# Tiles of h and f set 448 columns apart in SBUF, with the decoding states of the feed-forward convolution in the gaps

## The reference

```
h = rmsnorm(x, g_mix_pre); z = h @ w_in            # 1024 -> 24 column tiles and the gates
a = conv group (GLU, causal conv of width 31, group LayerNorm, silu)
hm = mLSTM group (4 heads, chunkwise)
x = x + rmsnorm(concat([a, hm]) @ w_out, g_mix_post)
up = rmsnorm(x, g_ffn_pre) @ w_up                  # 1024 -> 2 x 2816
up, ffn_buf_new = causal_dwconv(up, ffn_buf, w_conv_ffn, b_conv_ffn)   # width 3
f = gelu(up[..., :D_FF]) * up[..., D_FF:]
x = x + rmsnorm(f @ w_down, g_ffn_post)
x = x + (p @ w_ple) * sigmoid(rmsnorm(x, g_ple) @ w_ple_gate)
```

## Time and profile before

| | us |
|---|---|
| median of 3 runs (2684.24 to 2689.28) | 2686.83 |
| the profiled execution | 2685.84 |
| its span, first to last instruction | 2684.0 |
| PE busy, share of the span | 2655.4, 99% |
| PE's weight loads busy | 2581.4, 96% |
| DVE, ACT, POOL busy | 1726.9, 921.4, 237.1 |
| mean granted clock of TensorE | 0.998 |
| matmuls of L732 | 12960 |

### The profile page before, as it was taken

One profiled execution on the slowest core, in us unless ns is written; L12 is line 12 of the kernel. 1 busy time (PEld: TensorE's weight loads), 2 busy tenths in 40 slices (PEclk: granted clock), 3 DMA queues, 4 the chain that ended last, 5 costly groups with the idle time before them and its releaser, 6 DMA issues.

```text
span 2684.0 us, 37676 instructions
## 1 busy us (share of the span) xinstructions
PE 2655.4 (99%) x14541; PEld 2581.4 (96%) x14541; DVE 1726.9 (64%) x3699; ACT 921.4 (34%) x1932; POOL 237.1 (9%) x180
## 2 busy tenths in 40 slices
PE   9999999999999999999999999999999999999999
PEld 7989999999999999999999999999999998899998
DVE  7985898865566666555675664756866636472645
ACT  5464434464332122344321233542112425311113
POOL 4433515140000000000000000000000000000000
PEclk9999999999999999999999999999999999999999
DMA  9867999877566666565666666466666575466665
GB/s 331 321 222 293 359 335 365 315 282 285 188 233 233 233 234 234 216 239 210 227 233 233 234 234 256 182 226 233 229 233 232 216 284 146 179 240 229 235 233 204
DMA packets 125117, 660.59 MB, mean 246 GB/s; under 512 B 22010, under 2 KB 22654, under 8 KB 55182
## 3 DMA queue, kind: packets, MB, share of 16 engines
q1 hardware_dynamic: 111150, 628.29, 63.8%
q10 hardware_dynamic: 13792, 29.92, 3.3%
HBM read 533.04 MB, written 125.11 MB: 245 GB/s over the span
## 4 chain that ended last, share of the span: by engine, by line
PE 93%; DVE 4%; ACT 2%; DMA 1%; issue 1%; SPq 0%; DVEq 0%; ACTq 0%
PE proj L732 85%; PE m L732 1%; PE m L899 1%; PE m L932 1%; PE m L933 1%; PE m L893 1%; PE m L910 0%; PE m L761 0%; DMA w_split<-w_kept 0%; DVE small L1994 0%; PE m L952 0%; PE m L705 0%; PE m L704 0%; PE m L706 0%; PE m L865 0%
## 5 line engine op out<-in xcount | busy, mean ns | idle before, releaser
L732 PE MATMUL proj<-h_split,w_split 128*128 128x416 f32 x8112 | 1562.8, 352 | 4.5 <-DVE h_split L1831 2.1
L732 PEld LDWEIGHTS proj<-h_split,w_split 128*128 128x128 f32 x8112 | 1505.7, 188 | 20.1 <-issue 7.8
L732 PE MATMUL proj<-f_split,w_split 128*128 128x416 f32 x4584 | 880.8, 352 | 7.7 <-DMA w_split<-w_kept 2.2
L732 PEld LDWEIGHTS proj<-f_split,w_split 128*128 128x128 f32 x4584 | 851.5, 188 | 28.1 <-DVE f_split L2042 4.4
L1874 DVE SCALAR_TENSOR_TENSOR cv<-a_ext,vecs,cv 128x416 f32<-128x416 f32 (+1 forms) x480 | 302.5, 677 | 0.0
L1536 ACT ACTIVATE temp_room<-proj 128x416 f32<-128x416 f32 x176 | 91.3, 519 | 547.4 <-PE proj L732 547.3
L688 POOL TENSOR_TENSOR w_split<-w_raw,w_split 128x512 fp32r<-128x512 f32 x174 | 234.3, 1368 | 368.2 <-ACT w_split L1112 368.2
L2346 DVE SCALAR_TENSOR_TENSOR m<-temp_room,vecs,m 128x416 f32<-128x416 f32 (+1 forms) x440 | 256.8, 652 | 0.0
L2376 DVE TENSOR_TENSOR f_split<-m,f_split 128x416 fp32r<-128x416 f32 x110 | 65.1, 592 | 233.4 <-ACT f_split L1548 233.4
L2343 DVE TENSOR_SCALAR m<-temp_room,vecs 128x416 f32<-128x416 f32 (+1 forms) x220 | 145.9, 709 | 65.6 <-ACT temp_room L1536 65.5
L1750 DVE TENSOR_TENSOR mix_room<-mix_room,temp_room 128x416 f32<-128x416 f32 x131 | 81.0, 618 | 102.9 <-ACT temp_room L1130 97.2
(11 more groups left out here) (288 smaller groups left out, 1975.0 us busy)
## 6 DMA issues: line engine op xcount, KB each, us to landing
w_split<-w_kept SPq DMA_DIRECT2D x430, 1024.0 KB, 4.8
w_kept<-w_split SPq DMA_DIRECT2D x107, 1024.0 KB, 6.5
w_raw<-in_w_units SPq DMA_DIRECT2D x216, 256.0 KB, 4.7
x_resid<-in_x ACTq DMA_DIRECT2D x5, 1664.0 KB, 12.0
out_y<-x_resid ACTq DMA_DIRECT2D x8, 832.0 KB, 8.6
rows<-in_x ACTq DMA_DIRECT2D x4, 832.0 KB, 7.4
w_raw<-in_x ACTq DMA_DIRECT2D x3, 832.0 KB, 9.0
qkv<-in_p ACTq DMA_DIRECT2D x5, 416.0 KB, 5.9
```

What stands on the lines that cost most here:

```text
L732: ins = mm(to, home[:, low_w, b * P:b * P + P], act[:, n, low_a, :], start=n == 0 and not low_w and not low_a, stop=n == len(blocks) - 1 a ...
```

## The change

All 16 tiles of h, the 11 high tiles of f and its low tiles 0 to 4 begin 448 columns apart (`STEP`); f's low tiles 5 to 7 and 8 to 10 stay 416 apart. h grows from 6880 to 7168 columns, f from 9152 to 9632. The buffer `up_dec` (704 columns) is gone: the states of tile pairs 0 to 15 lie in the 16 gaps of h, those of 16 to 21 in the first six gaps behind f's high tiles. So the states are loaded by two DMAs of 16 and 6 pieces of 128 bytes per partition, and stored by two, where it was one of 2816 bytes per partition each way. What lay in f's room from high tile 8 on now begins at column 8 x 448. Every buffer behind f starts elsewhere: h by 1920 bytes, the weights and what follows by 3072 bytes.

```diff
+STEP = T + ROOM
...
-        f = Tiles(f_flat, [j * T for j in range(FH)], [(j + (2 * FH - KD if j < KD else FH - KD)) * T for j in range(FH)])
-        f_room = sb("f_room", [P, FH * 2 * T])
-        h_room = sb("h_split", [P, (KD - 1) * (T + ROOM) + T + KD * T], F32R)
-        h = Tiles(h_room, [k * (T + ROOM) for k in range(KD)], [(KD - 1) * (T + ROOM) + (k + 1) * T for k in range(KD)])
+        f_low, apart = FH * STEP, 4
+        f_size = f_low + (FH - KD) * T + apart * STEP + (KD - apart) * T
+        f = Tiles(f_flat, [j * STEP for j in range(FH)],
+                  [f_low + (FH - KD + j) * T + min(j, apart) * ROOM if j < KD else f_low + (j - KD) * T for j in range(FH)])
+        f_room = sb("f_room", [P, f_size])
+        f_late = KD * STEP
+        h_room = sb("h_room", [P, 2 * KD * STEP])
+        h = Tiles(h_flat, [k * STEP for k in range(KD)], [(KD + k) * STEP for k in range(KD)])
...
-        up_dec = sb("up_dec", [P, FT, 2, DEC_B, 2])
+        in_h = 2 * KD
+        up_dec_h = h_room[:, :].rearrange("p (j e) -> p j e", e=STEP)[:, :, T:]
+        up_dec_f = f_room[:, 0:(FT - in_h) * STEP].rearrange("p (j e) -> p j e", e=STEP)[:, :, T:]
...
+        def up_states(tensor):
+
+            flat = tensor.rearrange("p j n b r -> p j (n b r)")
+            return ((up_dec_h, flat[:, 0:in_h]), (up_dec_f, flat[:, in_h:FT]))
...
-                    final(t["up_s"], up_dec[:, :, :, :, :])
+                    for home, states in up_states(t["up_s"]):
+                        final(states, home)
...
-            for name, home in state_homes:
-                act.dma_start(home, t[name]).then_inc(s_states.sem, 16)
+            for home, states in state_homes:
+                act.dma_start(home, states).then_inc(s_states.sem, 16)
...
-                            ins = fn(dec[:, n, :, 0:2], up_dec[:, j, n, :, :], ACT.Copy)
+                            ins = fn(dec[:, n, :, 0:2], up_dec(j)[:, n, :, :], ACT.Copy)
...
-                            v.tensor_copy(up_dec[:, j, n, :, :], dec[:, :, DEC_S:])
+                            v.tensor_copy(up_dec(j)[:, n, :, :], dec[:, :, DEC_S:])
```

More of the change, by code:

```diff
@@ L301, in signal @@
             return Signal(ctx.enter_context(nc.semaphore(name)), per, ring, unit)
-        with nc.sbuf_tensor("f_split", [P, FH * 2 * T], F32R) as f_flat:
-            pass
-        f = Tiles(f_flat, [j * T for j in range(FH)], [(j + (2 * FH - KD if j < KD else FH - KD)) * T for j in range(FH)])
-        f_room = sb("f_room", [P, FH * 2 * T])
-        h_room = sb("h_split", [P, (KD - 1) * (T + ROOM) + T + KD * T], F32R)
-        h = Tiles(h_room, [k * (T + ROOM) for k in range(KD)], [(KD - 1) * (T + ROOM) + (k + 1) * T for k in range(KD)])
+        f_low, apart = FH * STEP, 4
+        f_size = f_low + (FH - KD) * T + apart * STEP + (KD - apart) * T
+        with nc.sbuf_tensor("f_split", [P, f_size], F32R) as f_flat:
+            pass
+        f = Tiles(f_flat, [j * STEP for j in range(FH)],
+                  [f_low + (FH - KD + j) * T + min(j, apart) * ROOM if j < KD else f_low + (j - KD) * T for j in range(FH)])
+        f_room = sb("f_room", [P, f_size])
+        f_late = KD * STEP
+        with nc.sbuf_tensor("h_split", [P, 2 * KD * STEP], F32R) as h_flat:
+            pass
+        h_room = sb("h_room", [P, 2 * KD * STEP])
+        h = Tiles(h_flat, [k * STEP for k in range(KD)], [(KD + k) * STEP for k in range(KD)])
         w = sb("w_split", [P, RING, 2, KD * P], F32R)
@@ L329, in hymba_layer, with up_dec @@
         up_tail = sb("up_tail", [P, FT, 2, 2])
-        up_dec = sb("up_dec", [P, FT, 2, DEC_B, 2])
+        in_h = 2 * KD
+        up_dec_h = h_room[:, :].rearrange("p (j e) -> p j e", e=STEP)[:, :, T:]
+        up_dec_f = f_room[:, 0:(FT - in_h) * STEP].rearrange("p (j e) -> p j e", e=STEP)[:, :, T:]
+        def up_dec(j):
+            piece = up_dec_h[:, j, :] if j < in_h else up_dec_f[:, j - in_h, :]
+            return piece.rearrange("p (n b r) -> p n b r", n=2, b=DEC_B)
+        def up_states(tensor):
+            flat = tensor.rearrange("p j n b r -> p j (n b r)")
+            return ((up_dec_h, flat[:, 0:in_h]), (up_dec_f, flat[:, in_h:FT]))
         vecs = sb("vecs", [P, NVEC])
@@ L345, in hymba_layer @@
         mixf = out_room[:, 4 * T:8 * T].rearrange("p (c t) -> p c t", c=4)
-        conv_tok = f_room[:, KD * T:KD * T + CT * 4 * P].rearrange("p (c n e) -> p c n e", c=CT, e=P)
+        conv_tok = f_room[:, f_late:f_late + CT * 4 * P].rearrange("p (c n e) -> p c n e", c=CT, e=P)
         w_raw_room = w_raw[:, :, :].rearrange("p r e -> p (r e)")
@@ L361, in hymba_layer @@
         c_homes = (mix_room[:, 1680:1680 + DEC_B * E1], rows[:, 0:4, :].rearrange("p r t -> p (r t)")[:, 0:DEC_B * E1],
-                   w_raw_room[:, 0:DEC_B * E1], f_room[:, KD * T:KD * T + DEC_B * E1])
+                   w_raw_room[:, 0:DEC_B * E1], f_room[:, f_late:f_late + DEC_B * E1])
         c_dec = [home.rearrange("p (b e) -> p b e", e=E1) for home in c_homes]
@@ L384, in hymba_layer @@
         x_next_w = w_raw_room[:, 0:4 * T].rearrange("p (r t) -> p r t", t=T)
-        sq_next = (mix_room[:, 4 * T:5 * T], mix_room[:, 6 * T:7 * T], f_room[:, (KD + 5) * T:(KD + 6) * T])
+        sq_next = (mix_room[:, 4 * T:5 * T], mix_room[:, 6 * T:7 * T], f_room[:, f_late + 5 * T:f_late + 6 * T])
         def x_next(i, mid=False):
@@ L428, in hymba_layer @@
         ahead = G_OUT + 3
-        ahead_home = f_flat[:, KD * T:KD * T + 2 * KD * P].rearrange("p (s e) -> p s e", s=2)
+        ahead_home = f_flat[:, f_late:f_late + 2 * KD * P].rearrange("p (s e) -> p s e", s=2)
         def split_home(u):
@@ L540, in hymba_layer @@
         n_const, n_late = 2, 4 + 2 * len(MASK_ROWS) + len(PIECES)
-        state_homes = (("up_dec", up_dec[:, :, :, :, :]), ("a_dec", a_dec[:, :, :, 0:CW - 1]))
+        state_homes = up_states(t["up_dec"]) + ((a_dec[:, :, :, 0:CW - 1], t["a_dec"]),)
         block = ctx.enter_context(nc.Block())
@@ L673, in _ @@
                 final(t["y"][last_blk, :, first:end], x[:, first:end, :])
-            sp.wait_ge(s_end.sem, 16 * (6 + len(Y_PIECES)))
+            sp.wait_ge(s_end.sem, 16 * (7 + len(Y_PIECES)))
             sp.wait_ge(s_yout.sem, s_yout.done(last_blk - 1, 1))
```

## The result

| | before | changed |
|---|---|---|
| median of the runs, us | 2687.73 (2684.24 to 2690.84, 16 runs) | 2693.64 (2688.45 to 2698.04, 16 runs) |
| ratio, 95% interval | 1 | 1.0019 (1.0012 to 1.0026) |
| profiled execution, us | 2685.84 | 2694.41 |
| its span, us | 2684.0 | 2692.6 |

The changed kernel is slower by 5.9 us, 0.2%, where 2679.0 us was forecast. That is small, but the interval leaves out 1, and the time lies above the range's end of 2687.

A forecast was written before the change was run, and what follows sets the result against it. PE's matmul stream, busy 99% of the span, was taken as the bound. Savings of 3.6 + 0.05 + 4.1 = 7.8 us, other costs 0, gave 2679.0 us against the median; range 2674 to 2687.

The forecast's parts named there:

- h, 2736 x 1.33 ns = 3.6 us less: h's matmuls on low tiles, a third of 8208, each save 1.33 ns by moving from 416 to 448 columns apart.
- a: Time of one PE matmul in sweeps over tiles 448 columns apart, reckoned at 186.85 ns.
- The distance: PE's sweeps over h and f: tiles 448 columns apart run 1.33 ns faster per matmul than tiles 416 apart.
- f, 4.1 us less: f's matmuls on high tiles and low tiles 0 to 4, 3808 in all, gain from 448; 4.2 to 5.1 us, taken as 4.1.
- The jumps between the sweeps: f's steps between high and low tiles: part of f's excess belongs to them and stays.
- Alignment against the weights: Rival: h's high and low tiles fall together with the weights modulo 256 bytes and slow; at most 33 us, 2716 us; chance 0.05.
- No change: Rival: distance is not the cause; 2686.8 us, up to 3 us less; chance 0.17, 0.25 with partial gain below measurement.
- Late loads: Rival: small state-store pieces delay the last weight loads, PE waits 3.3 us near the end; 2682.3 us; chance 0.08.
- the issue on ACT: Loading the states at the start: three DMAs for two keep ACT busy 0.83 us longer, hidden in 4.91 us idle; cost 0.
- the copies: ACT and DVE instructions reading and writing the states stay the same in number and size; cost 0.
- The bounds of 0.8 and 0.5 us: Upper costs: 0.8 us for loading states on ACT without cover, 0.5 us PE wait near the end from storing them.

The follow-up runs named there:

- e9: e6 with h's room placed ahead of f's, so h's high tiles lie 128 bytes off the weights modulo 256; 2687.70 us, ratio 0.9995.
- e6: The changed kernel with h's low tiles 416 columns apart again, its high tiles still 448 apart and level with the weights; 2695.82 us, ratio 1.0022.
- e10: The kernel before with 32 empty columns (128 bytes) ahead of the weights, h and f unmoved; 2692.25 us, ratio 1.0017.
- e1: The changed kernel with h's room placed ahead of f's, so h lies 128 bytes off the weights; 2692.65 us, ratio 1.0014.
- e3: The changed kernel with rooms ordered weights, f, h; f's high tiles level with the weights, h 128 bytes off; 2706.18 us, ratio 1.0062.
- e4: e1 with f's low tiles 0 to 3 moved on by 32 columns; 2690.48 us, ratio 1.0005.
- e13: e1 run again unaltered; 2692.15 us.
- e14: e1 run a third time unaltered; 2690.77 us.
- e16: e4 run again unaltered; 2693.39 us.
- e7: e9 with f's low tiles 0 to 3 moved on by 32 columns as in e4; 2684.35 us, ratio 0.9985.
- e15: e7 with 8 empty columns (32 bytes) ahead of the weights; 2734.64 us, ratio 1.0175.
- e8: The changed kernel with all of h's low tiles 32 columns nearer, still 448 apart; high tiles level, low ones 128 bytes off; 2695.98 us, ratio 1.0027.

## Why the prediction was wrong

The step that failed is the term "h, 2736 x 1.33 ns = 3.6 us less". It rests on a, the rate of tiles 448 apart, taken as a property of their distance alone: 186.85 ns. Measured, h became 0.56 to 0.64 ns slower per matmul in the two profiled executions, 4.5 and 5.1 us more. e9 against e6, and e10 against the kernel before, show why: the rate hangs on how the tiles lie to the weights as well, and the change's new sizes of f's and h's rooms put h level with the weights. The even sweeps of the earlier trace rows were even because of 448 and of the 128 bytes together. For all 16 tiles at 448 even that is not enough: with h 128 off, six executions (e1, e3, e4, e13, e14, e16) have h at 187.21 to 189.10 ns, and e1's ratio of 1.0014 is not clear of the change's 1.0019. That being level costs is shown where the low tiles are 416 apart; that a better place would have given the changed kernel its time back is not shown.

- *The distance.* That it plays a part was right. With h level, low tiles at 416 cost 6.9 us over the kernel before (e6), at 448 4.5 and 5.1 (the change). With h 128 bytes off, they take 187.21, 187.31 or 187.81 ns at 448, by execution (e1, e13, e14), 188.14 and 187.76 with four of f's low tiles moved (e4, e16) and 189.10 with the weights first (e3), against 187.49 at 416 (e9). Over 7910 matmuls the first three are 2.2 or 1.4 us saved, or 2.5 lost, and not 3.6 us saved, and the others lose 2.1 to 12.7: the forecast did not know of the 190.0 ns rhythm.
- *f, 4.1 us less.* It came to nothing: 188.18 before, 188.19 and 188.18 after. The step that failed is the same: 448 was taken to help wherever it was. It brought the high sweeps 0.25 ns, and the low sweeps, whose tiles 0 to 4 it made level with the weights, lost 1.2 ns. Moving low tiles 0 to 3 by 32 columns, and nothing else of f, took them off again and brought the 4.5 us in e7, with fewer distances of 448 than the change had. The jumps between the sweeps, which the prediction kept as a remainder, got cheaper with it (1.0 to 2.2 ns) and so did the sweeps (0.7 and 2.0 ns). Place and distance both changed in that edit, so their shares are not shown.
- *Alignment against the weights.* The rival had the mechanism, its place and its sign, and a chance of 0.05. Its point of decision, 0.5 ns for each matmul of h, is about what was measured; its price of 33 us was an upper bound, against some 5 us (e15, at another place, reached 50). The argument against it was bad: that every second low tile had lain level before, and in an uneven sweep, does not speak for being level. With one stretch of the stream even and no row of a room placed otherwise, 0.05 had nothing to rest on.
- *No change.* The Trainium skill, TensorE: Matmul & The Clock Gate, section Wait — 56ns, not 53.3ns?, gives the time of a warm matmul from start to start by its number of columns alone, an estimate of 175.8 ns here. The same stretch of h took from 186.7 ns (e1) to 191.9 ns (e15) a matmul here, and 8 or 32 empty columns were enough to move it, so a change of addresses alone does not leave the time as it is.
- *Late loads, the issue on ACT, the copies.* Costs of zero, as forecast. The queue times were underrated (2.94 us for the six pieces on ACT, 3.24 on SP), but the covers were wide enough. The bounds of 0.8 and 0.5 us were not used up.
- *Not foreseen:* 1.2 us in the first block's mixed part, between 130 and 149 us. It is there (1.2 to 1.8 us) in seven of the ten profiled executions of kernels with all of h 448 apart, but not in e3, e8 and e16, and at most 0.5 us with the low tiles at 416. What makes it is open.

Open as well: why e1's median is 4.5 us above that of the kernel before beside it (2692.65 and 2688.15), when the three profiled executions show h faster by 2.8 and 2.0 us or slower by 2.0. Waits of 2 to 3 us at 100 or 715 us and the low clock come and go between executions, and so few can't say how often. And why an address matters at all: whether the two reads meet in the memory, or something in PE's own queue, no run tells. That the place of the moving tile against the weights counts, and not that of either alone, e10 and e9 show together: e10 moved the weights and left h, e9 moved h and left the weights where they were modulo 256 bytes.

## What to carry to other kernels

When PE is busy for 99% of the span, as here, where a buffer ends is a parameter of the kernel. Before a change resizes or moves a buffer that is read by the matmuls, write down how the moving tiles and the weights lie to each other modulo 256 bytes, before and after, for every tile and not only the first, and keep that relation, with an empty piece if need be; then judge the change itself. And test the cause with the smallest edit that has only it: empty columns in the kernel before said in one run what several new orders of the rooms had left open.

## What the runs showed of the hardware

- 8 empty columns (32 bytes) ahead of the weights made the matmuls of 416 columns in the stream take some 191.9 ns in place of 187.4 in the mean, and the kernel 1.9% slower (e7 and e15).
- 32 empty columns (128 bytes) ahead of the weights took the h stretch from 98.89 to 99.44 us in the kernel before, with no tile moved (e10).
- A stream of matmuls can hold one of two rates, 186.7 or 190.0 ns, for 18 groups of 24, in different executions of one program (e1 and e14). In the sweeps shown the fast one has 349 ns for every matmul, the slow one 346 to 356.
- The clock fell to its lower level for a few us in the last block, at up to three places, in some executions of a kernel and not in others; 16 small products then took 3.23 us in place of 1.96. It fell elsewhere too: at 105 us in e16, behind a wait of 2.74 us, and at 720 us in e6, behind one of 1.94 us, while a wait of 2.12 us at the same place in e13 left it at the upper level.
